# Start, ring refill and last expert of a two-block kernel: fewer warming products, first slot refilled by units, residual put into the accumulators

## The reference

```python
gates, idx = lax.top_k(jnp.swapaxes(aff, 1, 2), cap)      # 16 experts, cap = 32 tokens each
xs = h[idx]                                               # tokens gathered for each expert
gu = xs @ wgu                                             # 32 x 1024 by 1024 x 4096
ga, up = split(gu); y = (silu(ga) * up) @ wd              # by 2048 x 1024
moe = zeros.at[idx].add(gates[..., None] * y)
x = x + moe
return x * rsqrt(mean(x * x) + eps) * final_norm_g
```

## Time and profile before

| | us |
|---|---|
| median of 3 runs | 1516.22 |
| the runs | 1511.03 to 1517.49 |
| profiled execution | 1512.67 |
| its span, first to last instruction | 1510.9 |
| PE busy | 1183.1 |
| DVE busy | 445.0 |
| ACT busy | 380.5 |

### The profile page before, as it was taken

One profiled execution on the slowest core, in us unless ns is written; L12 is line 12 of the kernel. 1 busy time (PEld: TensorE's weight loads), 2 busy tenths in 40 slices (PEclk: granted clock), 3 DMA queues, 4 the chain that ended last, 5 costly groups with the idle time before them and its releaser, 6 DMA issues.

```text
span 1510.9 us, 20178 instructions
## 1 busy us (share of the span) xinstructions
PE 1183.1 (78%) x8814; PEld 777.4 (51%) x8814; DVE 445.0 (29%) x874; ACT 380.5 (25%) x841; POOL 88.2 (6%) x98
## 2 busy tenths in 40 slices
PE   9999999999997997896657666566666666566655
PEld 8998989999976876442312223223223223123212
DVE  5565776545688855010000000000000000000002
ACT  5655566444555644110000000000000000000002
POOL 0000020000135412000000000000000000000001
PEclk9999999999998999898887888888788788888787
DMA  7436546564553259899999999999999999999996
GB/s 289 167 135 222 174 189 220 184 251 168 183 205 131 98 223 394 367 434 429 431 430 429 430 432 432 430 432 430 431 429 431 429 432 433 430 432 432 429 425 270
DMA packets 34201, 503.88 MB, mean 333 GB/s; under 512 B 4673, under 2 KB 5313, under 8 KB 8770
## 3 DMA queue, kind: packets, MB, share of 16 engines
q1 hardware_dynamic: 30240, 493.70, 78.6%
q10 hardware_dynamic: 3874, 8.90, 1.7%
HBM read 501.54 MB, written 1.05 MB: 333 GB/s over the span
## 4 chain that ended last, share of the span: by engine, by line
PE 66%; another core or an unknown queue 15%; DMA 7%; DVE 4%; issue 3%; ACT 3%; POOL 1%; ACTq 0%; DVEq 0%; POOLq 0%
PE PB L99 64%; DMA RING<-in_wdn_dram 6%; PE PB L102 2%; DVE SPL L108 1%; POOL SPL L108 1%; DVE SG L108 1%; ACT SPH L105 1%; DMA AG<-in_ag_dram 1%; ACT SG L105 1%; DVE CO L116 0%; POOL SM L136 0%; POOL SP L112 0%; DVE XN L116 0%; DVE BC L125 0%
## 5 line engine op out<-in xcount | busy, mean ns | idle before, releaser
L99 PE MATMUL PB<-RING,XS 128*32 128x512 f32 x2048 | 325.3, 785 | 178.8 <-DMA RING<-in_wgu_dram 174.8
L99 PEld LDWEIGHTS PB<-RING,XS 128*32 128x32 f32 x2048 | 72.3, 136 | 386.0 <-DMA RING<-in_wgu_dram 211.4
L99 PE MATMUL PB<-RING,HHT 128*32 128x256 f32 x2048 | 159.3, 471 | 88.3 <-DMA RING<-in_wdn_dram 86.7
L108 DVE TENSOR_TENSOR SPL<-RAW,SPH 128x512 fp32r<-128x512 f32 x306 | 202.7, 721 | 38.0 <-ACT SPH L105 35.8
L99 PE MATMUL PB<-XTH,SPL 128*128 128x256 f32 x704 | 201.7, 287 | 0.0
L99 PE MATMUL PB<-XTH,SPH 128*128 128x256 f32 x704 | 199.2, 283 | 0.0
L99 PE MATMUL PB<-XTL,SPH 128*128 128x256 f32 x704 | 199.1, 283 | 0.0
L105 ACT ACTIVATE SPH<-RAW 128x512 fp32r<-128x512 f32 x340 | 186.6, 621 | 5.4 <-DMA RAW<-in_wst_dram 2.0
L99 PEld LDWEIGHTS PB<-RING,HHT 128*32 128x32 f32 x2048 | 74.0, 132 | 155.0 <-DMA RING<-in_wdn_dram 93.2
L105 ACT ACTIVATE SG<-PB 128x512 f32<-128x512 f32 x16 | 9.6, 597 | 548.7 <-PE PB L99 548.7
L99 PEld LDWEIGHTS PB<-XTL,SPH 128*128 128x128 f32 x704 | 135.0, 192 | 0.5
(11 more groups left out here) (301 smaller groups left out, 1371.8 us busy)
## 6 DMA issues: line engine op xcount, KB each, us to landing
RING<-in_wgu_dram SPq DMA_DIRECT2D x56, 4096.0 KB, 52.9
RING<-in_wdn_dram SPq DMA_DIRECT2D x28, 4096.0 KB, 52.9
RAW<-in_wst_dram SPq DMA_DIRECT2D x84, 1024.0 KB, 4.9
RING<-in_wgu_dram SPq DMA_DIRECT2D x11, 2048.0 KB, 50.4
RING<-in_wdn_dram SPq DMA_DIRECT2D x7, 2048.0 KB, 21.1
RING<-in_wgu_dram SPq DMA_DIRECT2D x10, 1024.0 KB, 6.8
RAW<-in_wst_dram SPq DMA_DIRECT2D x4, 256.0 KB, 5.5
MEM<-in_mem_dram ACTq DMA_DIRECT2D x1, 1024.0 KB, 7.3
```

The lines of the kernel that those rows point to most:

```text
L99: return pe.do(lambda e: e.matmul(out_, lhsT, rhs, start=start, stop=stop), after)
L108: return on.do(lambda e: e.tensor_tensor(out_, a, b, op), after)
```

## The change

- 24, 8 and 8 warming products become 6, 1 and 4.
- In expert 0, group 0, each chunk's products release a load of that 1 MB for expert 1 (`ring_unit`), where one load of 4 MB followed the last chunk.
- In expert 0, PE first writes X into the accumulators by identity products, so that they begin with the residual.
- In expert 15, output quarter m's products are cut in two and `combine(15, m - 1)` is issued between the halves. The accumulators of quarters 2 and 3 are closed after expert 14, copied to XL and put back by identity products, quarter 3 in banks 0 and 1.
- `keep_busy` makes products of the identity in expert 15: 6 after each of k = 2 to 6, 5 at the start of `expert_hidden`, 4 after output quarters 0 and 1.
- At the end, squares and gain products read PSUM, with no addition to X; the sums of both tiles are reduced and raised to -1/2 in one instruction each; the four stores go out on two queues, ACT's and SP's.

```diff
-    for _ in range(24):
+    for _ in range(6):
         w = mm(PB[4][:, 0:P], WARM[:, :], WARM[:, :], True, True, warm_ok)
     for i in range(2):
         g_mix = mm(PB[6 + i][:, :], WARM[0:1, :], GROW[:, halves[i]], True, True, row_in)
-    for _ in range(8):
-        w = mm(PB[4][:, 0:P], WARM[:, :], WARM[:, :], True, True)
+    w = mm(PB[4][:, 0:P], WARM[:, :], WARM[:, :], True, True)
...
     t0 = turn(XN, 0, n0, (0, 1))
-    for _ in range(8):
+    for _ in range(4):
...
+    def ring_unit(q, after):
+        slot = SLOT_OF[0]
+        c = slice(UNIT * q, UNIT * q + UNIT)
+        note(1, 0, q, 1, [load(sp, RING[slot][:, c], weights_of(1, 0)[:, c], s_second[q], 16, after)])
...
-        if e < 14:
+        if e == 0 and g == 0:
+            ring_unit(q, w)
+        elif e < 14:
...
-        refill(n, w)
+            refill(n, w)
         xs_read[e] = w
...
     def expert_hidden(e, w):
+        if e == 15:
+            keep_busy(3, 5)
...
+    def keep_busy(b, n):
+        for _ in range(n):
+            w = mm(PB[b][:, 0:P], ident, ident, True, True, *held[b])
+        return w
...
+            if between and i == 0:
+                between()
...
+        late = e == 15 and m >= 2
+        banks = [t if late and m == 3 else 4 + 2 * t + m // 2 for t in range(2)]
+        for t, b in enumerate(banks):
+            if late:
+                mm(PB[b][:, c], ident, XL[:, t, c], True, False, x_late[t], *held[b])
+            elif e == 0 and m % 2 == 0:
+                mm(PB[b][:, :], ident, X[:, t, T * m:T * m + 512], True, False, *held[b])
...
+            res = combine(e - 1, 3, y)
+            if e == 15:
+                x_late = [copy(XL[:, t, :], PB[5 + 2 * t][:, :], res[t]) for t in range(2)]
...
+                if e == 15 and 2 <= k < KD - 1:
+                    keep_busy(2, 6)
...
-    for m in range(3):
-        res = combine(15, m, expert_out(15, m, h))
...
+    def settle(t, i, c, src, w):
+        def squares(after):
+            st["sg"] = act(SG[:, 0:c.stop - c.start], src, ACT.Square, after, st["sg"], scale=1.0 / 32, accum_out=MS3[:, t, i:i + 1])
+            return st["sg"]
+        def scaled(after):
+            yg[t].append(tt(YG[:, t, c], src, GF[:, c], ALU.mult, after, g_fin, gu_done))
+            return yg[t][-1]
+        if t:
+            squares(scaled(w))
+        else:
+            scaled(squares(w))
+    def finish_part(m, y):
+        res = combine(15, m, y)
+        if m:
+            for t in range(2):
+                c = slice(0, 512) if m == 1 else slice(512, 768)
+                settle(t, m - 1, c, PB[4 + 2 * t + m // 2][:, 0:c.stop - c.start], res[t])
+    ys = []
+    for m in range(4):
+        between = (lambda: finish_part(m - 1, ys[m - 1])) if m else None
+        ys.append(expert_out(15, m, h, between))
+        if m in (0, 1):
+            keep_busy(0, 4)
+    res = combine(15, 3, ys[3])
...
+    q0 = act(SG[:, 0:T], last[0], ACT.Square, res[0], st["sg"], scale=1.0 / 32, accum_out=MS3[:, 0, 2:3])
+    x1 = copy(SQ[:, :], last[1], res[1])
+    q1 = ttr(XL[:, 1, 0:T], SQ[:, :], SQ[:, :], 1.0 / D, 0.0, ALU.mult, ALU.add, MS3[:, 1, 2:3], x1)
+    s2 = reduce(total, MS3[:, :, :], ALU.add, q0, q1, eps_ok)
+    for t in (1, 0):
+        yg[t].append(tt(YG[:, t, c], SQ[:, :] if t else last[0], GF[:, c], ALU.mult, x1 if t else q0, g_fin, gu_done))
+    r_ok = power(r_all, total, s2)
...
+            line, y = (sp, YG[:, t, c]) if i else (act_l, YG[:, t, c])
```

More of the change, by code:

```diff
@@ L279, in build @@
     IOTA = place("IOTA", [P, T], F32, at(29))
+    XL = place("XL", [P, 2, 512], F32, at(23))
     SQ = place("SQ", [P, T], F32, at(30))
@@ L850, in build @@
     s_fill = {}
+    s_second = [sem(f"s_second{i}") for i in range(4)]
     s_half = [sem(f"s_half{i}") for i in range(NS)]
@@ L872, in ring_load @@
         slot = SLOT_OF[g]
-        note(e, g, 0, 4, [load(sp, RING[slot][:, :], weights_of(e, g), s_r[slot], 16 * e, after)])
+        note(e, g, 0, 4, [load(sp, RING[slot][:, :], weights_of(e, g), s_r[slot], 16 * (e - (g == 0)), after)])
+    def ring_unit(q, after):
+        slot = SLOT_OF[0]
+        c = slice(UNIT * q, UNIT * q + UNIT)
+        note(1, 0, q, 1, [load(sp, RING[slot][:, c], weights_of(1, 0)[:, c], s_second[q], 16, after)])
     def ring_half(g, h, after):
@@ L877, in ring_half @@
         c = slice(2 * UNIT * h, 2 * UNIT * h + 2 * UNIT)
-        got = (s_half[slot], 16) if h else (s_r[slot], 16 * 15)
+        got = (s_half[slot], 16) if h else (s_r[slot], 16 * (15 - (g == 0)))
         note(15, g, 2 * h, 2, [load(sp, RING[slot][:, c], weights_of(15, g)[:, c], *got, after)])
@@ L1619, in expert_hidden, with expert_out @@
         return h
-    def expert_out(e, m, h):
+    def keep_busy(b, n):
+        for _ in range(n):
+            w = mm(PB[b][:, 0:P], ident, ident, True, True, *held[b])
+        return w
+    def expert_out(e, m, h, between=None):
         b = 3 - m % 2
@@ L1645, in combine @@
         g, c = GT[e % 2], slice(T * (m % 2), T * (m % 2) + T)
+        late = e == 15 and m >= 2
[5 more added lines that the diff above has]
+                mm(PB[b][:, :], ident, X[:, t, T * m:T * m + 512], True, False, *held[b])
         res = []
-        for t in range(2):
-            own = e == 15 and m == 3
-            b = t if own else 4 + 2 * t + m // 2
+        for t, b in enumerate(banks):
             x = slice(t * P, (t + 1) * P)
-            mm(PB[b][:, c], g[:, x], YL[m % 2][:, :], own or (e == 0 and m % 2 == 0), False, *y, st["g"], *held[b])
-            res.append(mm(PB[b][:, c], g[:, x], YH[m % 2][:, :], False, own or (e == 15 and m in (1, 2))))
+            mm(PB[b][:, c], g[:, x], YL[m % 2][:, :], False, False, *y, st["g"])
+            res.append(mm(PB[b][:, c], g[:, x], YH[m % 2][:, :], False, late or (e, m) in ((14, 3), (15, 1))))
         st["y", m % 2] = res[1]
@@ L1663, in row_columns @@
         return a
+    MS3 = small(8).rearrange("p (t i) -> p t i", t=2)
+    eps_ok = fill(MS3[:, :, 3:4], EPS)
     gather_first(0)
@@ L1674, in build @@
             w = expert_in(e, 0)
-            combine(e - 1, 3, y)
+            res = combine(e - 1, 3, y)
+            if e == 15:
+                x_late = [copy(XL[:, t, :], PB[5 + 2 * t][:, :], res[t]) for t in range(2)]
             for k in range(1, KD):
@@ L1690, in build @@
     g_fin = load(act_l, GF[:, :], row("final_norm_g_2", D), sem("s_gf"), 16, gu_done)
[L1691 to L1705, removed]
@@ L1707, in gained @@
-    def gained(t, m, a, on):
-        c = slice(T * m, T * m + T)
-        yg[t].append(tt(YG[:, t, c], X[:, t, c], GF[:, c], ALU.mult, a, g_fin, gu_done, on=on))
-    for m in range(3):
-        res = combine(15, m, expert_out(15, m, h))
[L1713 to L1731, removed]
+    total, r_all = small(2), small(2)
+    yg = [[], []]
+    def settle(t, i, c, src, w):
[9 more added lines that the diff above has]
+            scaled(squares(w))
@@ new lines, in build @@
+    c = slice(3 * T, 4 * T)
+    last = [PB[t][:, T:2 * T] for t in range(2)]
+    q0 = act(SG[:, 0:T], last[0], ACT.Square, res[0], st["sg"], scale=1.0 / 32, accum_out=MS3[:, 0, 2:3])
[4 more added lines that the diff above has]
+        yg[t].append(tt(YG[:, t, c], SQ[:, :] if t else last[0], GF[:, c], ALU.mult, x1 if t else q0, g_fin, gu_done))
@@ L1735, in build @@
             c = slice(512 * i, 512 * i + 512)
+            line, y = (sp, YG[:, t, c]) if i else (act_l, YG[:, t, c])
             if i:
-                o = act(YG[:, t, c], YG[:, t, c], ACT.Copy, r[t][1], *yg[t], scale=r[t][0])
+                o = ts(y, y, r_all[:, t:t + 1], None, ALU.mult, None, r_ok, *yg[t])
             else:
-                o = ts(YG[:, t, c], YG[:, t, c], r[t][0], None, ALU.mult, None, r[t][1], *yg[t])
+                o = act(y, y, ACT.Copy, r_ok, *yg[t], scale=r_all[:, t:t + 1])
             n_out += 16
-            load(sp, out[t * P:(t + 1) * P, c], YG[:, t, c], s_out, n_out, o)
+            load(line, out[t * P:(t + 1) * P, c], y, s_out, n_out, o)
     sp.do(lambda e: e.nop(), [Load(s_out, n_out)])
```

## The result

The changed kernel takes 1506.58 us (median of 8 runs, 1504.78 to 1507.71), the kernel before 1513.35 in the 8 runs that stand beside them (1511.03 to 1517.57). The ratio is 0.995, its 95% interval 0.9936 to 0.9964. The change makes the kernel faster, by 6.8 us between the medians. That is 0.45%, a little under the 0.5% (7.6 us) that the prediction named as what a measurement can tell from no change; with eight runs of each kernel the interval still leaves out 1. The forecast was 1505.0.

What follows compares the result with a forecast made beforehand. PE was taken to bound 13 to 500 us, transfers 660 to 1490, then a chain of small steps. Gains 4.3 + 3.9 + 1.0 = 9.2 us gave 1503.5 or 1507.0; the middle, 1505, was predicted, range 1499 to 1511.

Steps and rivals of the forecast that it cites:

- likeliest case: Whole kernel: the forecast of 1505 us, with its own range 1500 to 1509 and chance 0.63.
- Part 1: Start of the kernel: fewer warming products let the first real product come earlier, 4.3 us gained (3.2 to 5.4).
- Part 3: Last expert: `combine` between the halves of an output quarter's products shortens the tail, 1.0 us gained.
- base of 1514.4: Whole kernel: the time before the change from which the forecast of 1505 us was taken.
- term of 4.3: Start: 4.0 us from an earlier `first_norm` plus 0.3 us up to the second unit's products.
- best case of 6.3: Start: earliest time in us for `first_norm`, with `g_mix` at the high clock; 8.2 at worst, 7.4 taken.
- Part 2: First slot's refill: 1 MB loads shrink the hole in the weight stream, 3.9 us gained (3.65 to 4.8).
- 0.7 plus 1.15: Weight stream after the first filling: us still missing, 0.7 in the shrunken hole and 1.15 at the next refill.
- second hole: Weight stream behind the four 1 MB loads: a smaller hole can open before the next refill flows, 1.15 us.
- squares in the way: Last expert: ACT's squares ahead of YH, with the low clock, leave YH only 0.4 us earlier; 1.0 taken.
- the tail gives it back: Rival, end: squares ahead of YH and low clock lose 1 to 2 us; total 1507.5, chance 0.10.
- What would show it: Signs in the trace: `first_norm` near 7.4 us, first product near 10.9, no empty window, DMA share 1.00 to about 1482.

Runs made afterwards that it cites:

- e1: Only the fewer warming products (6, 1 and 4), on the kernel before: 1508.17 us, ratio 0.9974.
- a2: The whole changed kernel run again without an edit, against the kernel before: 1507.54 us, ratio 0.9964.
- e7: The changed kernel with no warming products at all: 1507.80 us, ratio 0.9969 to the kernel before.
- e3: Only the whole last part (residual in accumulators, interleaved combines, `keep_busy`, new norm and stores), on the kernel before: 1514.21 us, ratio 1.0006.
- e2: Only the first slot refilled by four 1 MB loads, on the kernel before: 1511.61 us, ratio 0.9992.
- e4: Fewer warming products and the 1 MB loads with the old end, on the kernel before: 1507.01 us, ratio 0.9963.
- e4b: Fewer warming products and the 1 MB loads with the old end, run again on the kernel before: 1506.76 us, ratio 0.996.
- e9: The changed kernel with the identity products of quarters 2 and 3 issued early: 1508.04 us, ratio 0.9972 to the kernel before.
- e8: The changed kernel with squares after the next quarter's YH and YL, identity products early, stores reordered: 1506.14 us, ratio 0.9953 to the kernel before.
- e6: The changed kernel without the products of `keep_busy`: 1507.48 us, ratio 0.9965 to the kernel before.
- e5: The changed kernel with a quarter's squares and gain products after YH and YL of the next: 1505.38 us, ratio 0.995 to the kernel before.
- e11: e8 with each tile's last factor worked out by itself and both last squares on ACT: 1506.34 us, ratio 0.9953 to the kernel before.

## Why the prediction was right or wrong

**Direction and size: right.** 1506.58 lies in the likeliest case's own range. Taken from the profiled execution, as the sum was made, 9.2 us were forecast and 7.5 measured; between the medians it is 6.8. That the number came within 1.6 us is in part luck: part 1 gave 1.0 us more than forecast and part 3 lost 1.5 where 1.0 was to be gained, and a base that was too high made up for some of the gain that was missing. The three runs known then had a high median; with 57 runs of the kernel before, its medians are 1512.1 to 1513.4, and 9 of the runs lie at 1516 to 1518. That is why the base of 1514.4 was 1 us above the median of 1513.35.

**Part 1: the mechanism right, its size within the bounds but not one number.** e1 shows that a start earlier by 5.4 us stays earlier by as much to the end of the span. The term of 4.3 rested on a rise of the clock at 6.6 us; in the profiled execution the clock rose during `g_mix`, which took 2.24 us, so `first_norm` came at 6.53, near the best case of 6.3. In a2 it took 3.78, and the part was worth 3.8 us (606.77 to 602.98). Of the ten traces with six products, five have expert 0 at 601.4 to 601.7 and five at 602.6 to 603.4: 3.4 to 5.4 us under the trace before, within the bounds of the prediction. The two levels are those of `g_mix`: 1.98 to 2.24 us in the first five, 3.77 or 3.78 in the others. The three traces with 24 products themselves lie at 605.9, 606.8 and 607.6, so a difference of two traces is uncertain by a microsecond or so. By the Trainium skill (TensorE: Matmul & The Clock Gate, What's actually happening) the low clock is the default until activity releases it; the traces agree in that e7, with nothing ahead of `g_mix`, has the low clock's 3.78 us there.

**Part 2: the hole right, what it is worth too high.** The units do what was worked out. Summed over windows of 2 us for 28 us, the transfers miss 1.8 to 2.5 us around the place in six traces with units, 5.2 to 5.7 in three without. The prediction's own sum was 0.7 plus 1.15, or 1.85, with a second hole behind it. In place of the second hole only a shallow dip came, 307 GB/s in the window from 610 to 612. By the rule of the Trainium skill (DMA: Bandwidth & Descriptors, Measured (HBM→SBUF, 128 partitions, SWDGE, issued from GpSimd)) the four units would have lost an estimated 10 us; the trace disagrees, since no window is empty and only 2.1 us are missing in all, though the five windows from 602 to 612 do average 337 GB/s, below the stream's 430. What was missed stands at the other end of the stream, of whose ragged end the prediction said that nothing in the diff changes it. The 16 parts of a load don't land together. Worked out from the records of landings, from the end of the first filling to the last load's first and last part:

| profiled executions | first part landed, us | last part landed, us | between |
|---|---|---|---|
| 3 without units (before, e1, e3) | 879.7 to 880.2 | 887.9 to 888.4 | 8.2 to 8.3 |
| 11 with units, mean | 876.0 | 885.7 | 9.8 |
| 11 with units, range | 875.1 to 876.6 | 884.6 to 886.8 | 8.4 to 10.6 |

The first part gained 3.9 us, just as forecast; the last part, without which the load can't be used, 2.4 on average. In none of the fourteen traces is this last load what PE waited for: quarter 3's second half, which uses it, starts 0.16 us or more after its last part. The load that does release the tail is quarter 2's, the 2 MB at the head of expert 15's last slot; quarter 2's first product follows its last part by 0.04 to 0.05 us in nine of the traces. By the same working that last part came 2.6 us earlier on average (880.6 instead of 883.2). The changed kernel's profiled execution, with 3.7 us, has the smallest spread of the eleven. Why the parts drift further apart with units in the queue was not tried. In the medians part 2 is worth even less: 1.0 us between e2 and before, 1.2 between e4 and e1. In the traces of e2 and e4b quarter 3 at the low clock takes another 1.4 us; whether that is so in most of their runs the times don't tell.

**Part 3: the step that failed.** The prediction put `combine` between the halves down as 1.0 us of gain, with the squares in the way as its small counterweight (-0.4 at worst). The rival "the tail gives it back" had the price, and the traces decide for it. From quarter 2's first product to quarter 3's YH, quarter 2 at the high clock, it takes 7.48 us in a2 and 7.49 in e9, with the squares ahead of YH, and 5.80 in e8, with the squares behind it: 1.7 us that the order of two calls costs (1.9 us between the medians of e9 and e8). With the low clock in quarter 2 it is 8.50. The old end needed 7.42 with quarter 2 at the low clock, and 8.35 in e4b (1487.09 to 1495.44) with quarter 3 at it; at the high clock's 1.93 for 3.35 that would be 6.9. That is an estimate from one execution. By it, at equal clock, the changed end is about 0.6 us longer than the old one up to this YH, and with the squares behind YH it is 1.1 shorter. How much of that 1.1 is the interleaving stays open, since at the high clock the old end has its own squares ahead of quarter 2's YH, by 1.27 us in e4b (1489.02 to 1490.29): interleaving alone, against an old end with its squares moved, was not tried and may earn next to nothing. e9 clears the identity products; what `keep_busy` is worth stays open (e6). After YH nothing was counted, within 0.5 either way; it became 0.4 longer. e3, e4 and e4b say the same in times: the last part gains nothing that could be measured.

With the squares behind YH there is little left to take from this stretch: in e5, e8 and e11 quarter 3's second half starts 0.16 to 0.19 us after the last landing. Removing one wait of this tail brings the next one near.

**What would show it** had named this: "YH of quarter 3 more than 2 us behind the last landing" is 3.6 us (1490.8 to 1494.42). As a sign it was weak, since the kernel before has 2.5 (1499.8 to 1502.34); with the squares behind YH it is 1.3 in e5 and 1.4 in e8. `first_norm` and the first product came a little earlier than named, the window without bytes is gone, and the share holds 1.00 to 1482 less 0.02 in the last window of it.

## What to carry to other kernels

On an engine that runs its list in order, work that nobody waits for (here the squares) must be issued behind the step on which the last chain hangs, above all where it has a wait of its own on another engine. When a hole in a stream of transfers is closed, look at when the last parts of the loads that the end uses land, not at the mean rate: here 3.9 us were saved for the first part of the last load, 2.4 for its last part and 2.6 for that of the load that releases the tail. Test each part of a change by itself: the smallest edit, three loop counts, gave 4.5 of the 6.8 us, and the longest gave nothing that could be measured.

## What the runs showed of the hardware that was not expected

- **The start has two outcomes from the same instructions.** With six warming products `g_mix`, four one-row records, took 1.98 to 2.24 us in five traces (the changed kernel's first, e1, e4, e4b, e5) or 3.77 to 3.78 in five others (a2, e6, e8, e9, e11), where expert 0 comes 0.9 to 2.0 us later. In the three traces with 24 products it took 1.98 each time.
- **The parts of one load land 8 to 11 us apart at the end of a stream of some 880 us.** The last part bounds when the last quarter's products can start; in the changed kernel the last 8 us of transfers run at 166 to 272 GB/s.
- **The clock level in the last two quarters differs from execution to execution.** Quarter 3's 32 records took 1.93 us or 3.35 to 3.38 in kernels that have the same end (1.93 in e4, the longer ones in e4b and e2).
- **GpSimd's power of two columns at once took 0.84 us.** Two single ones had taken 1.24 together (from 1505.23 on in the trace before) and took 1.12 in e11, but the first tile no longer goes ahead of the second.
